# Cross attention: inverse roots through logarithm and exponential, with earlier exponentials and later sums

## The reference

```python
def _rms_norm(x, g):
    y = xf * lax.rsqrt(jnp.mean(xf * xf, axis=-1, keepdims=True) + EPS)
    return y * g

def _memory_cross_attention(h, mem_n, wq, wkv, q_g, k_g, wo):     # 4 heads of 128, M = 256
    q = _rms_norm((h @ wq).reshape(B, T, X_HEADS, X_HEAD_DIM), q_g)
    k, v = jnp.split(mem_n @ wkv, 2, axis=-1)
    k = _rms_norm(k.reshape(B, M, X_HEADS, X_HEAD_DIM), k_g)
    s = jnp.einsum('bthd,bmhd->bhtm', q, k) / math.sqrt(X_HEAD_DIM)
    p = jax.nn.softmax(s, axis=-1)
    o = jnp.einsum('bhtm,bmhd->bthd', p, v)
    return o.reshape(B, T, X_HEADS * X_HEAD_DIM) @ wo

h = h + _memory_cross_attention(_rms_norm(h, norm_xattn[l]), _rms_norm(mem, mem_norm[l]), ...)
h = h + 0.5 * _swiglu(_rms_norm(h, norm_ffn2[l]), ffn2_wi[l], ffn2_wo[l])
```

## Time and profile before

| | |
|---|---|
| runs | 2672.66 us median of 3 (2670.84 to 2676.19) |
| the profiled execution, its own time | 2668.24 us |
| its span, from first to last instruction | 2666.5 us |
| PE / DVE / ACT / POOL busy | 99% / 43% / 41% / 46% |
| granted TensorE clock | 1.00 |
| cross attention with output projection, layer one | from about 892 to 976 us in the span |
| the same, layer two | from about 2213 to 2297 us |

### The profile page before, as it was taken

The page is one execution under the profiler, slowest core; times in us unless marked ns, Lnnn a source line. Parts: engine busy times, 40 slices in busy tenths (PEclk is TensorE's granted clock), DMA queues, the critical chain, the costliest instruction groups (busy, mean ns, idle before and its releaser), DMA issues.

```text
span 2666.5 us, 35749 instructions
## 1 busy us (share of the span) xinstructions
PE 2626.6 (99%) x12597; PEld 2105.8 (79%) x12597; DVE 1142.3 (43%) x1813; ACT 1089.0 (41%) x1674; POOL 1231.0 (46%) x616
## 2 busy tenths in 40 slices
PE   8999999999999999999999999999999999999999
PEld 7888888866778778888888888887667787788887
DVE  3221258966535542121331212698664364421212
ACT  5322242367644554222342222424675445532222
POOL 4444456772234344444444444577522353444443
PEclk9999999999999999999999999999999999999999
DMA  4334334321233223333333343333212332333332
GB/s 136 103 95 119 99 95 111 76 60 51 59 87 113 81 79 111 95 95 98 92 103 95 95 123 93 105 103 72 60 50 58 99 107 79 87 103 95 97 100 79
DMA packets 474694, 243.75 MB, mean 91 GB/s; under 512 B 41052, under 2 KB 466886, under 8 KB 474566
## 3 DMA queue, kind: packets, MB, share of 16 engines
q1 hardware_dynamic: 474542, 242.04, 32.3%
q10 hardware_dynamic: 24, 0.01, 0.0%
HBM read 237.79 MB, written 2.10 MB: 90 GB/s over the span
## 4 chain that ended last, share of the span: by engine, by line
PE 63%; issue 17%; POOL 9%; DVE 4%; POOLq 3%; ACT 3%; DVEq 1%; DMA 1%; ACTq 0%; SPq 0%
PE pg L707 19%; PE pg L710 18%; PE pg L713 18%; POOL wL L656 9%; PE pA L1004 1%; POOLq L683 1%; PE pA L829 1%; PE pA L951 1%; POOLq L685 1%; PE pg L734 1%; DVE convb L1894 1%; ACT wH L1262 1%; PE pg L1225 1%; PE pg L1223 1%; PE pg L1224 1%
## 5 line engine op out<-in xcount | busy, mean ns | idle before, releaser
L656 POOL TENSOR_TENSOR wL<-raw,wH 128x1024 fp32r<-128x1024 f32 (+1 forms) x472 | 1088.7, 2308 | 1402.0 <-ACT wH L1262 1398.4
L1262 ACT ACTIVATE wH<-raw 128x1024 fp32r<-128x1024 f32 (+1 forms) x472 | 477.3, 1012 | 1128.5 <-PE pg L713 959.9
L707 PE MATMUL pg<-gxH,wH 128*128 128x512 f32 (+1 forms) x2288 | 896.0, 392 | 1.8 <-DVE big L1961 0.8
L713 PE MATMUL pg<-gxH,wL 128*128 128x512 f32 (+1 forms) x2288 | 892.2, 390 | 0.0
L710 PE MATMUL pg<-gxL,wH 128*128 128x512 f32 (+1 forms) x2288 | 887.3, 388 | 0.0
L707 PEld LDWEIGHTS pg<-gxH,wH 128*128 128x128 f32 x2288 | 429.9, 188 | 101.8 <-issue 14.7
L713 PEld LDWEIGHTS pg<-gxH,wL 128*128 128x128 f32 x2288 | 429.9, 188 | 89.6 <-issue 4.4
L710 PEld LDWEIGHTS pg<-gxL,wH 128*128 128x128 f32 x2288 | 430.0, 188 | 87.2 <-issue 3.5
L713 PE MATMUL pg<-hH,wL 128*128 128x512 f32 x1008 | 398.3, 395 | 0.0
L707 PE MATMUL pg<-hH,wH 128*128 128x512 f32 x1008 | 398.1, 395 | 0.0
L710 PE MATMUL pg<-hL,wH 128*128 128x512 f32 x1008 | 396.0, 393 | 0.0
(11 more groups left out here) (270 smaller groups left out, 2219.7 us busy)
## 6 DMA issues: line engine op xcount, KB each, us to landing
raw<-in_ffn_wi SPq DMA_DIRECT2D x352, 256.0 KB, 3.1
raw<-in_w_in SPq DMA_DIRECT2D x200, 256.0 KB, 3.2
raw<-in_ffn_wo SPq DMA_DIRECT2D x128, 256.0 KB, 3.0
raw<-in_ffn_wo SPq DMA_DIRECT2D x64, 192.0 KB, 2.6
raw<-in_xkv SPq DMA_DIRECT2D x32, 256.0 KB, 3.0
raw<-in_w_out SPq DMA_DIRECT2D x32, 256.0 KB, 3.0
raw<-in_sgu_out SPq DMA_DIRECT2D x32, 128.0 KB, 2.3
raw<-in_conv_out SPq DMA_DIRECT2D x32, 128.0 KB, 2.2
```

The lines of the kernel that those rows point to most:

```text
L656: pool.tensor_tensor(wL[:, s % 4, 0:n, :], raw[:, s % 2, 0:n, :], wH[:, s % 4, 0:n, :].bitcast(F32), ALU.subtract)\
L707: mm(o, wH[:, s, k, :], rh(k), start=(k == 0), stop=False)
L713: last = mm(o, wL[:, s, k, :], rh(k), start=False, stop=(k == kt - 1))
L1262: return act.activation(o, i, ACT.Copy, **kw)
```

## The change

It does five things, all on the cross attention but the last:

- `x_root` takes a logarithm and an exponential with scale -0.5 in place of a square root; between the two ACT drains. `x_max` turns that estimate r of the inverse root into r (1.5 - 0.5 v r r), one Newton step, in place of a reciprocal.
- The operands of that step, `x_var`, `x_sqr` and `x_neg` (the maxima, `xnm` before), lie in PSUM, in `pO`. `x_mean` makes `xvar` in one operation in place of two, and writes the variance twice, to `x_var` and to `xsc`.
- On ACT the exponentials of heads 1 and 2 come ahead of the second `x_turned_out` of the head before, and those of head 3 ahead of `ahead(l, U_XV + 1)`.
- On PE the sums of head 0 come after 15 matmuls of the second query unit, not after nine, and so behind the scores of head 0 (after twelve).
- `stat(l, 15)` of the second FFN comes after 19 matmuls of its unit, not after 14.

```diff
-        xnm = sb("xnm", [P, 4, TT])
+        x_var, x_sqr, x_neg = [pO[:, 16 * i:16 * i + 16].rearrange("p (h c) -> p h c", h=4)
+                               for i in range(3)]
...
-                                 between=within(14, lambda: stat(l, s_norm, ones))
+                                 between=within(19, lambda: stat(l, s_norm, ones))
...
                 def beside_queries(j, p):
                     if j >= 1:
-                        if p == 2:
+                        if p == (4 if j == 1 else 2):
                             x_norms(j - 1)
                         if p == 3:
                             x_scores(j - 1)
...
                 def x_root(h):
                     act.wait_ge(xst_out, risen(xst_out, l, XSTEP["z", h] + 1))
-                    act.activation(xsc[:, h, :], xsc[:, h, :], ACT.Sqrt).then_inc(x_rt, 1)
+                    act.activation(xsc[:, h, :], xsc[:, h, :], ACT.Ln)
+                    act.drain()
+                    act.activation(xsc[:, h, :], xsc[:, h, :], ACT.Exp, scale=-0.5)\
+                        .then_inc(x_rt, 1)
...
                 x_turned_out(0, 0)
+                x_exps(1)
                 x_turned_out(0, 1)
                 x_square(2)
-                x_exps(1)
                 ahead(l, U_XQ + 3)
                 x_root(2)
                 x_turned_out(1, 0)
+                x_exps(2)
                 x_turned_out(1, 1)
                 x_square(3)
-                x_exps(2)
                 ahead(l, U_XV)
                 x_root(3)
                 x_turned_out(2, 0)
+                x_exps(3)
                 ahead(l, U_XV + 1)
-                x_exps(3)
                 x_turned_out(2, 1)
...
                     if h == 0:
-                        TS(xvar[:, :], pT[:, 0:4], 1.0 / D, EPS, ALU.mult, ALU.add)
+                        TS(xvar[:, :], pT[:, 0:4], EPS / D, EPS * EPS, ALU.mult, ALU.add)
                         dve.drain()
-                        TS(xvar[:, :], xvar[:, :], EPS, None, ALU.mult)
-                        dve.drain()
+                    STT(x_var[:, h, :], pT[:, 4:8], 1.0 / XDH, xvar[:, :], ALU.mult, ALU.add)
                     STT(xsc[:, h, :], pT[:, 4:8], 1.0 / XDH, xvar[:, :], ALU.mult, ALU.add)\
                         .then_inc(xst_out, 1)
...
-                        dve.tensor_reduce(xnm[:, h, 2 * half:2 * half + 2],
+                        dve.tensor_reduce(x_neg[:, h, 2 * half:2 * half + 2],
...
                     dve.wait_ge(x_rt, risen(x_rt, l, h + 1))
-                    dve.reciprocal(xsc[:, h, :], xsc[:, h, :])
+                    TTt(x_sqr[:, h, :], x_var[:, h, :], xsc[:, h, :], ALU.mult)
                     dve.drain()
-                    TTt(xb[:, h, :], xnm[:, h, :], xsc[:, h, :], ALU.mult).then_inc(x_b, 1)
+                    STT(x_sqr[:, h, :], x_sqr[:, h, :], -0.5, xsc[:, h, :], ALU.mult, ALU.mult)
+                    dve.drain()
+                    STT(xsc[:, h, :], x_sqr[:, h, :], 1.5, xsc[:, h, :], ALU.add, ALU.mult)
+                    dve.drain()
+                    TTt(xb[:, h, :], x_neg[:, h, :], xsc[:, h, :], ALU.mult).then_inc(x_b, 1)
```

## The result

| | before | after |
|---|---|---|
| runs | 2672.39 us median of 20 (2666.66 to 2679.34) | 2677.68 us median of 20 (2672.17 to 2680.40) |
| the profiled execution | 2668.24 us, span 2666.5, mean granted clock 1.000 | 2678.47 us, span 2676.8, mean granted clock 0.996 |

The ratio is 1.0017, with a 95% interval of 1.0010 to 1.0024: 4.5 us slower (5.3 by the medians). The forecast was 1.0 us slower and "no change that can be told". It falls inside the 0.2%, but 3.5 us of it stand in no term of the sum. Lines of the kernel after are 1 to 4 higher (829 is 830, 1127 is 1128, 1139 is 1140, 1640 is 1641 and 1643).

The account below looks back on a forecast made before the run. It took TensorE, busy 99% of the span, as the bound. Per layer +1.8 - 2.6 + 2.4 - 1.1 = +0.5, +1.0 us for two, gave 2669.3 profiled and, 4.4 higher, a median of 2673.7 us; range 2667 to 2680.

Parts of the forecast that it names:

- Norm sums later: Cross attention, heads 0 and 1: waits of 0.71 and 2.46 us replace 1.38 us, +1.8 us per layer.
- Last transposes: Head 3: moved exponentials delay a weight copy, so PE waits 4.1 us for 0.97 + 0.68, +2.4 per layer.
- the chain of rows 5: ACT copy of an output-projection weight tile, POOL subtraction, next load, its ACT copy, then PE's last transposes: 8.8 us.
- designed gain kept: Rival, chance 0.09: the weight load does not bind head 3's last transposes; -3.1 us per layer, 2666.4 us.
- Statistic: Last FFN's norm statistic: five more matmuls in front, 1.13 us of work, cover a 1.11 us wait; -1.1 per layer.
- Two loads per head: ACT's root: one 1.28 us table load before the logarithm, one between it and the exponential, none before the softmax exponentials.
- one table: Rival, chance 0.13: one load serves logarithm and exponential, head 0's root 1.3 us earlier; 0.6 less per layer, 2672.5 us.
- dearer switch: Rival, chance 0.05: a table load costs 2.6 us, so roots end after the maxima; 1.4 more per layer, 2676.4 us.
- Newton in the loop: Rival, chance 0.11: DVE's small PSUM operations have pitch 0.5, not 0.24; a layer is +4.6 - 1.1, 2679.7 us.
- Exponentials earlier: Scores of heads 2 and 3: moved exponentials are done in time, 2 x 0.26 replaces 2 x 1.56, -2.6 per layer.
- an idle time shown before PE costs that much plus 0.16: Every PE wait: its cost is the shown idle time plus 0.16 us, because matmul rows overlap by 0.16.
- the 4.4 us: Whole kernel: the median of runs lies 4.4 us above the profiled execution, added to 2669.3 to give 2673.7.

Follow-up runs that it names:

- the kernels with the sums back, with and without the copy ahead: The change with head 0's norm sums after nine matmuls: 2673.35 us, 0.9996; also with the weight copy ahead of head 3's root: 2660.31 us, 0.9959.
- One table: The change plus one explicit load, ahead of head 0's root, of the table set holding logarithm and exponential: 2673.11 us, ratio 1.0005 to the kernel before.
- the exponentials back in their old place: The change with only the exponentials of heads 1 and 2 back behind the second copy and the square: 2678.84 us, ratio 1.0026 to the kernel before.
- the root alone: The kernel before with only the new root, Newton step and PSUM operands, the order and places as before: 2669.14 us, ratio 0.9991.
- the idle time filled: The change with unused matmuls in PE's waits, nine before head 1's sums, sixteen before head 3's last transposes: 2671.81 us, ratio 0.9986 to the kernel before.
- the table of executions: 72 executions of the unchanged kernel before, grouped by mean granted clock: medians from 2668.2 us at 1.000 to 2677.7 us at 0.995.

## Why the prediction was right, and where it was short

**The forecast and its range held.** A change within 0.2%, and the measured 2677.7 lies in 2667 to 2680, 4 us above the value.

**Norm sums later, +1.8: right.** Waits of 0.7 and 2.20 in place of those forecast; undone, they went. **Last transposes, +2.4: right**, with a wait of 4.1 as said and the chain of rows 5 behind it; the rival "designed gain kept" fell, and the kernels with the sums back, with and without the copy ahead, show that without this chain the wait is gone. **Statistic, -1.1: right**, alone and in the whole. **Two loads per head, nothing behind a load, and a Newton step at 0.24: right**; the rivals "one table", "dearer switch" and "Newton in the loop" are decided by the rows of ACT and DVE. One table may have been worth more (1.0005 against 1.0017, some 3 us, but the intervals overlap) than the 1.2 us that I gave it.

**Exponentials earlier, -2.6: the sum right by luck, the reason wrong.** The waits at the scores of heads 2 and 3 did go (and the 0.26 at the sums that I left in their place did not come), but not because of the move: with the exponentials back in their old place they stayed away, and with the root alone they went. They were the load of the exponential's table, 1.28 us ahead of the first exponential. My part on tables had the load move off that place, and I did not ask what that alone would give.

**The step that failed** is the first one: "an idle time shown before PE costs that much plus 0.16". It costs more wherever the granted clock falls behind it, a cost that the sum put at nothing: 3.3 us behind the wait of 2.20 at the sums of head 1. With the idle time filled the sum holds to 0.3 us per layer. The change replaces seven waits per layer of 0.4 to 1.4 us with one of 0.7, one of 2.2 and one of 4.2, nearly the same sum, and has a mean clock of 0.9959 where the kernel before has 0.9976; by the table of executions (9.5 us between 1.000 and 0.995) 0.0017 is some 3.3 us, about the missing part. The forecast fell inside its range because that part was smaller than the range, not because the sum had it.

**A second step of the same kind:** I carried the 4.4 us between the profiled execution and the median over as a constant. It is no constant. By the table of executions it is what the clock cost the kernel before in a median run. The profiled execution, at 1.000, was one without that cost, and a change of the order can change it: at the first norm sums, at the sums of head 1 and at the last transposes. It also falls in the mixers, which no kernel here changes.

## What to carry to other kernels

A wait of TensorE can have a price beyond its length: work at half the clock behind it, in some executions. Short waits are not safe from it: two of 0.47 and 0.38 us around norm sums were followed by it in ten of 16 places, one of 3.9 to 5.2 at the last transposes in all eight. A kernel whose profiled execution is among its fastest should be read beside the clocks of its other runs. Before a step is moved ahead of another in an engine's order, follow what hangs on the one that is passed: here a weight copy of 1.06 us began a chain of 8.8 us, and moving it up, with the norm sums back in their place, turned a loss of 4.5 us into a gain of 11, of which 10 are the copy's (0.9996 to 0.9959). And when a function is replaced, ask which table loads leave which places, before crediting a move that is made beside it.

## What was unexpected of the hardware

The same wait did not always bring the clock down. Layer two of the same execution of the kernel after has the same idle time of 2.2 us at the sums of head 1, and the stretch around it shows full clock:

```profile
2240.00:2243.00 3.00, 1.90 (x13) 1.78 (x14) 1.55 (x7) 2.88 (x5) 1.02 (x1) 1.00 0.00 0
...
2277.00:2282.00 5.00, 4.76 (x10) 2.26 (x11) 0.00 (x0) 2.21 (x5) 2.13 (x1) 0.66 0.32 95
```

There it fell only behind the wait of 4.1 (0.66 is a mean over 1.00 and 0.50), and the layer lost 1.7 us beyond its waits (2.2 less 0.5) where layer one lost 5.4. Over the kept traces the wait of 2.2 at the sums of head 1 was followed by 0.50 in three of six places, the waits of 2.1 to 2.4 in the mixers in nine of 15, and those of 1.40 us at the scores in none of eight. What else decides it, the traces don't tell; what they show is that the cost is one of an average over executions. And useless work can be worth its place: 24 matmuls that nothing reads made the kernel before 0.19% faster, by a way that no trace here shows.
